# A two-layer hybrid decoder trunk on 8 cores: the first weight loads wait for input tiles, the operand sums stand in the order of use, and the planner's settings change

## The chip, the cores and the metric

The kernel runs on the 8 cores of one Trainium2 chip. A core has TensorE (PE, matrix products; PEld is its weight load), VectorE (DVE), ScalarE (ACT), GpSimd (POOL) and SyncE (SP), and 16 DMA engines that all queues of the core share. Each core computes 2 of the 16 sequences from start to end; nothing is exchanged between cores. The metric is the device time of the slowest core in microseconds (us); a lower number is better.

## The reference

```python
for l in range(DEPTH):                                   # DEPTH = 2
    x = x + 0.5 * swiglu(rms_norm(x, ffn1_norm[l]), ffn1_w1[l], ffn1_w3[l], ffn1_w2[l])
    x = x + token_mixing(rms_norm(x, mix_norm[l]), w_in[l], ...)
    x = x + 0.5 * swiglu(rms_norm(x, ffn2_norm[l]), ffn2_w1[l], ffn2_w3[l], ffn2_w2[l])

def rms_norm(x, g):
    return x * rsqrt(mean(x * x, axis=-1) + EPS) * g

def swiglu(h, w1, w3, w2):
    return (silu(h @ w1) * (h @ w3)) @ w2

def token_mixing(h, ...):
    u = h @ w_in
    # four groups of 256 columns: sparse attention (compressed, selected and
    # window branches), gated short convolution, window attention with sinks,
    # causal pooling; then a norm per group and
    return y @ w_out
```

The width is 1024, a sequence has 2048 tokens, the feed-forward width is 2816, x is float32.

## The kernel before

**Units.** The feed-forward work is cut into 16 units of 1024 tokens (sequence s, half u, layer l, which of the two feed-forwards fi). The list FL holds their order: units 0 to 3 are the four halves under the first feed-forward of layer 0. The mixer runs in 16 chunks of 512 tokens, woven into units 4 and later by the list MIX, and starts once units 0 and 1 have been recorded. A unit first normalises its two 512-token halves (`norm`: 8 input tiles of 128 features are loaded, squared on ACT at L630, summed on PE at L632 against ones, turned into a factor on ACT at L644 and L646, and scaled on DVE at L639).

**Products.** Every matrix product is made by a Strassen-like scheme of 7 products on quarters (`PROD`, L734) in the place of 8. Its operands are sums of quarters: `tops` (L713) makes t1 to t4 of the activations on DVE at L717, `wsum` (L677) makes the sums of the weights on DVE at L681. Product 1 and 2 need only activations of the first half; product 5 needs t1, which needs both halves. A `pair` (L738) takes two weight tiles (w1 and w3 of one q) and runs 14 products of 4 matmuls, 56 matmuls at L725; a unit has 11 pairs, then 4 `dcq` steps of 77 matmuls with three w2 tiles each, whose results POOL adds to yT in memory with an accumulating DMA (L824). So a unit is 11 x 56 + 4 x 77 = 924 matmuls at L725.

**Weights.** The weights lie in memory as float32. At its first use a tile is loaded by POOL's queue, which casts it to float16 (`prep`, L657 and L659), gets one DVE sum, and SP's queue stores it to a scratch tensor (L666); later units load it from there with SP (`wload`, L692). A tile is 128 x 2048 float16, 512 KB; pool "4" holds N4 of them at once. `PREP` = (a, b) says which share a/b of the tiles of a later feed-forward is prepared ahead, in the background of an earlier unit (`preps`, L1425); (0, 1) means none. Unit 0's w2 tiles are loaded, used and not stored; they are prepared again in unit 1.

**Start.** The first two norms load x by SP (L627, 256 KB each, 16 loads). `ycopy` (L1386) copies x to yT by SP, 512 KB each, 8 for a unit. Unit 0's first weight tile is asked for between its two norms; the next tiles as the pairs are recorded.

**What sets the order.** All operations are recorded by `op`, with their tiles, into a Graph. `schedule` then places them by a list planner: it takes the earliest-recorded ready operation of each engine, looks at most `ahead` operations past PE's front, hands out the slots of the pools, and holds a DMA back while more than `win` modelled bytes are under way (a wait for the landing of an earlier DMA is then built in). ACT stays with its current function table up to `hold` us. The result is one fixed, in-order list for each engine, with waits on semaphores between them. A waiting instruction stops everything behind it on its engine.

```python
                op("sp" if wide else "pool", lambda e, kc=kc: e.dma_start(out=xa(xf[kc]), in_=src[s, :, kc, c * 512:(c + 1) * 512]),
...
                        early["13", 0, 0] = mk("13", 0, 0)
```

## Time and profile before

| what | value |
|---|---|
| median of 3 runs | 4681.64 us (4676.58 to 4685.83) |
| the profiled execution, its time | 4662.98 us |
| its span, slowest of 8 cores (core 6) | 4661.9 us |
| spans of the 8 cores | 4636.2 to 4661.9 us |
| PE busy | 4518.3 us (97%) |
| DVE busy | 3088.4 us (66%) |
| ACT busy | 3050.7 us (65%) |
| PE idle in the first 40 us | 33.9 of 40 us |

A profile is one execution. Its time lies 18.7 us below the median of the three timed runs, so differences are worked out against the profile and then set against the median. In the rows below, "start us, us" are from the span's start; a bracket gives the engine's idle time before the instruction and what ended it; a window's row gives the busy time of each engine in that stretch, then the granted clock of PE as a share, the busy share of the 16 DMA engines and what they moved.

### The profile page before, as it was taken

What the parts mean: (1) busy time and instruction counts of PE and PEld (TensorE: products, weight loads), DVE (VectorE), ACT (ScalarE), POOL (GpSimd) and SP (SyncE); (2) the same over time, 40 slices, a digit from 0 to 9 for tenths busy, and PEclk for the clock granted to TensorE, in tenths of its full rate; (3) what the DMA queues carried; (4) which work ended last, traced back from release to release, by engine and by line L of the source; (5) the groups of instructions that cost most, each with busy time, mean ns of one, the idle gap of its engine ahead of it and who ended that gap; (6) DMA issues with size and microseconds to landing.
All of it is one profiled execution on the core that took longest, in us unless ns stands there. A gap on an engine that the chain in (4) does not pass through costs nothing.

```text
span 4661.9 us, 86720 instructions; the slowest of 8 cores (4636.2 to 4661.9 us)
## 1 busy us (share of the span) xinstructions
PE 4518.3 (97%) x25524; PEld 2101.8 (45%) x25524; DVE 3088.4 (66%) x7506; ACT 3050.7 (65%) x5742; POOL 874.4 (19%) x1282
## 2 busy tenths in 40 slices
PE   5899899999999999989999999999999999999999
PEld 2344444444444444444444444444444444444444
DVE  4656576667677667675757775766676767666663
ACT  3444577586877585867947666759585868585542
POOL 0011121111212112211122212111122221111101
PEclk9999999999999999999999999999999999999999
DMA  9998796767998759886588666664776898646554
GB/s 190 184 202 195 164 196 125 173 132 148 166 210 169 158 111 193 174 166 143 139 170 178 128 156 136 141 139 93 172 170 126 190 180 178 142 99 141 130 126 92
DMA packets 365404, 725.20 MB, mean 156 GB/s; under 512 B 37776, under 2 KB 145424, under 8 KB 364944
## 3 DMA queue, kind: packets, MB, share of 16 engines
q0 software_dynamic: 173904, 290.78, 44.3%
q1 hardware_dynamic: 191040, 428.87, 29.2%
q8 instruction: 218, 3.57, 0.3%
q14 instruction: 242, 1.98, 0.2%
HBM read 615.37 MB, written 256.43 MB: 187 GB/s over the span
## 4 chain that ended last, share of the span: by engine, by line
PE 85%; DMA 6%; DVE 4%; issue 3%; ACT 2%; POOL 0%; SPq 0%; DVEq 0%; ACTq 0%; POOLq 0%
PE ps L725 61%; PE ps L885 8%; PE ps L1167 4%; PE ps L1182 4%; PE ps L1195 2%; DMA yT<-M 2%; PE ps L632 1%; DMA M<-xT 1%; PE ps L1031 1%; DVE M L639 1%; DMA M<-s 1%; DMA M<-w2r 1%; DVE M L717 1%; PE ps L949 1%; PE ps L1276 1%
## 5 line engine op out<-in xcount | busy, mean ns | idle before, releaser
L725 PE MATMUL ps<-M 128*128 128x512 f16 x14784 | 3422.9, 380 | 54.5 <-DVE M L772 13.2
L725 PEld LDWEIGHTS ps<-M 128*128 128x128 f16 x14784 | 1409.0, 98 | 1730.8 <-issue 170.0
L681 DVE TENSOR_TENSOR M<-M 128x512 f16<-128x512 f16 (+1 forms) x1780 | 691.8, 412 | 130.7 <-DMA M<-s 53.8
L772 DVE TENSOR_TENSOR M<-M,ps 128x512 f16<-128x512 f32 x704 | 481.5, 685 | 435.6 <-PE ps L725 320.8
L824 POOL DMA_DIRECT2D yT<-M x464 | 400.3, 884 | 1697.2 <-ACT M L812 826.8
L776 ACT COPY M<-ps 128x512 f32<-128x512 f32 x704 | 410.1, 584 | 249.8 <-PE ps L725 241.7
L1185 ACT ACTIVATE M<-ps 128x512 bf16<-128x512 f32 x824 | 455.0, 603 | 51.0 <-PE ps L1182 47.1
L885 PE MATMUL ps<-M 128*128 128x512 f16 x1920 | 449.1, 380 | 8.9 <-DMA M<-hin 5.7
L732 ACT COPY ps<-ps 128x512 f32<-128x512 f32 x468 | 272.2, 582 | 213.1 <-PE ps L725 158.8
L717 DVE TENSOR_TENSOR M<-M 128x512 f16<-128x512 f16 x960 | 388.3, 424 | 34.3 <-DVE M L717 1.1
L764 DVE TENSOR_TENSOR M<-M,ps 128x512 f16<-128x512 f16 x352 | 240.9, 684 | 208.6 <-PE ps L725 206.5
L818 DVE SCALAR_TENSOR_TENSOR M<-ps,M 128x512 f32<-128x512 f32 x232 | 159.6, 689 | 279.2 <-PE ps L725 231.7
L812 ACT ACTIVATE M<-ps 128x512 f32<-128x512 f32 x232 | 138.7, 598 | 231.8 <-PE ps L725 225.5
L885 PEld LDWEIGHTS ps<-M 128*128 128x128 f16 x1920 | 184.7, 98 | 225.4 <-issue 13.8
L639 DVE SCALAR_TENSOR_TENSOR M<-M,GN 128x512 f16<-128x512 f16 (+1 forms) x384 | 265.2, 745 | 21.4 <-ACT M L646 21.2
L1182 PE MATMUL ps<-M 96*128 96x512 f16 x824 | 272.7, 380 | 2.0 <-DVE M L1215 0.9
L760 ACT ACTIVATE M<-M 128x512 f16<-128x512 f16 x352 | 219.1, 629 | 77.5 <-DVE M L772 76.0
L627 POOL DMA_DIRECT2D M<-yT x320 | 181.6, 608 | 458.5 <-PE ps L725 60.1
L756 ACT ACTIVATE M<-ps 128x512 f16<-128x512 f32 x352 | 209.5, 595 | 77.7 <-PE ps L725 74.2
L630 ACT ACTIVATE M<-M 128x512 bf16<-128x512 f16 (+1 forms) x384 | 228.1, 627 | 39.1 <-DMA M<-xT 34.8
L1195 PEld LDWEIGHTS ps<-M 128*128 128x128 bf16 x3296 | 173.8, 97 | 135.5 <-issue 26.4
L1167 PE MATMUL ps<-M 128*128 128x512 f16 x1024 | 233.7, 379 | 0.4 <-DVE M L1383 0.4
(152 smaller groups left out, 3903.2 us busy)
## 6 DMA issues: line engine op xcount, KB each, us to landing
M<-s SPq DMA_DIRECT2D x360, 512.0 KB, 5.8
yT<-M POOLq DMA_DIRECT2D x592, 256.0 KB, 9.3
s<-M SPq DMA_DIRECT2D x120, 512.0 KB, 7.8
M<-hin SPq DMA_DIRECT2D x210, 256.0 KB, 7.6
M<-w13r POOLq DMA_DIRECT2D x88, 512.0 KB, 11.9
M<-yT POOLq DMA_DIRECT2D x320, 128.0 KB, 7.0
M<-hout SPq DMA_DIRECT2D x112, 256.0 KB, 6.2
M<-w2r POOLq DMA_DIRECT2D x40, 512.0 KB, 8.3
```

Of the source, the lines that this page charges most:

```text
L639: op("dve", lambda e, d=dst[kc], gi=gi, x=xf[kc]: e.scalar_tensor_tensor(out=p1(d)[:, 0:512], in0=xa(x), scalar=GN[:, gi:gi + 1], in1=p2f( ...
L681: op("dve", lambda e, o_=o_, a_=a_, b_=b_, al=al: e.tensor_tensor(out=wap(W, o_, w), in0=wap(W, a_, w), in1=wap(W, b_, w), op=al), reads=[ ...
L717: op("dve", lambda e, o_=o_, x_=x_, y_=y_: e.tensor_tensor(out=p1(o_)[:, 0:512], in0=p1(x_)[:, 0:512], in1=p1(y_)[:, 0:512], op=ALU.subtract),
L725: r = e.matmul(ps(bk)[:], lhsT=wap(w, pos, 128, j * 128), rhs=p1(B[n, k0 + j])[:, 0:512], start=start and j == 0, stop=stop and j == nk - ...
L732: op("act", lambda e: e.copy(out=ps(dst)[:], in_=ps(src)[:]), reads=[src], writes=[dst], dur=0.57)
L772: op("dve", lambda e: e.tensor_tensor(out=p1(dst)[:, 0:512], in0=p2f(t), in1=ps(bk)[:], op=ALU.add), reads=[t, bk], writes=[dst], dur=t_dv ...
L776: op("act", lambda e: e.copy(out=p2f(t), in_=ps(bk)[:]), reads=[bk], writes=[t], dur=0.6)
L824: op("pool", lambda e: e.dma_start(out=yT[s, :, dc, t0:t0 + 512], in_=p2f(o), accum_op=ALU.add), reads=[o], writes=[kY[s][dc][2 * u + hf]] ...
L885: r = e.matmul(ps(bk)[:], lhsT=p2(t)[:, kc * 128:(kc + 1) * 128], rhs=p1(xn[kc])[:, 0:512], start=kc == 0, stop=kc == 7, skip_group_check= ...
L1167: r = e.matmul(ps(bk)[:], lhsT=p2(wo)[:, kc * 128:(kc + 1) * 128], rhs=yap(kc), start=n == 0, stop=n == 7, skip_group_check=True)
L1182: op("pe", lambda e: e.matmul(ps(sbk)[:], lhsT=kap(), rhs=p4(Q)[0:kk, b * 512:(b + 1) * 512], start=True, stop=True, skip_group_check=True ...
L1185: op("act", lambda e: e.activation(out=p1b(et)[:, 0:512], in_=ps(sbk)[:], func=AF.Exp, scale=0.125), reads=[sbk], writes=[et], dur=0.65, t ...
```

## The change

Four things. The first 16 weight loads get a `gate`, an extra dependency: the first waits for the landing of the sixth x load, the second for the twelfth, the others for the sixteenth. `tops` makes t3 and t1 of all four k first and then t2 and t4. PREP becomes (1, 3): every third tile of a later feed-forward is prepared one to four units ahead. And numbers of the planner change (pool sizes N1, N2, N4, look-ahead, window, hold, the modelled issue time of a weight load), so the whole order is made anew.

```diff
-        self.ahead = 400
+        self.ahead = 600
...
-        self.win = 5000000.0
+        self.win = 4000000.0
...
-        self.hold = 4.0
+        self.hold = 5.0
...
-    def op(self, eng, fn, reads=(), writes=(), dur=0.1, tbl=None, dma=0, after=(), prio=None, lat=0.0, look=None):
+    def op(self, eng, fn, reads=(), writes=(), dur=0.1, tbl=None, dma=0, after=(), prio=None, lat=0.0, look=None, gate=None):
...
+        if gate is not None:
+            deps.add(gate)
...
-N1, N2, N4, NS, NPF, NPX = 130, 20, 7, 24, 4, 4
-LOOKM, LOOKC = 250, 20
+N1, N2, N4, NS, NPF, NPX = 128, 19, 8, 24, 4, 4
+LOOKM, LOOKC = 250, 100
+XGATE = (5, 11, 15)
...
-MIX, PREP = ((2.0, 0.0), (5.0, 4.4), (14.4, 16.0)), (0, 1)
+MIX, PREP = ((2.0, 0.0), (5.0, 4.4), (14.4, 16.0)), (1, 3)
...
+                xloads.append(o)
...
-                op("pool", lambda e: e.dma_start(out=p4(t), in_=src), writes=[(t, (0, 1, 2, 3))], dur=0.8, dma=1048576)
+                op("pool", lambda e: e.dma_start(out=p4(t), in_=src), writes=[(t, (0, 1, 2, 3))], dur=0.6, dma=1048576, gate=gate)
...
-            for k in range(4):
-                tops(B, k)
+            tops(B, range(4))
             return B
 
-        def tops(B, k):
-            t3, t2, t4 = tile("1"), tile("1"), tile("1")
-            b11, b12, b21, b22 = (B[n, k] for n in ("11", "12", "21", "22"))
-            for o_, x_, y_ in ((t3, b22, b12), (b12, b12, b11), (t2, b22, b12), (t4, b21, t2)):
...
+        def tops(B, ks):
+            for k in ks:
+                B["t3", k], B["t2", k], B["t4", k] = tile("1"), tile("1"), tile("1")
+                B["t1", k] = B["12", k]
+            for names in (("t3", "t1"), ("t2", "t4")):
+                for k in ks:
+                    for o in names:
+                        x, y = dict(t3=("22", "12"), t1=("12", "11"), t2=("22", "t1"), t4=("21", "t2"))[o]
...
+                    gate = None
+                    if n == 0 and w == "13" and q < 8:
+                        gate = xloads[XGATE[min(2 * q + j, 2)]]
+                    return prep(l, fi, w, q, j, True, True, gate)
```

All other instructions keep their number: PE 25524, DVE 7506 and POOL 1282 in both kernels. SP issues 36 DMAs more, 24 loads of 512 KB and 12 of 384 KB from scratch (L692 before, L698 after): the tiles that PREP now prepares ahead.

POOL's queue at the start of the program, before. M4 is the pool of weight tiles, w13r the float32 weights; s1, s5, s8 and s10 are semaphores of landings, s31 the first of PE's.

```order
L599 MEMSET ZT 128x512 [waits barrier_Pool_Activation_PE_DVE_SP_gather]
L657 DMA M4<-w13r 128x2048 x3
L657 DMA M4<-w13r 128x2048 [waits s1]
L657 DMA M4<-w13r 128x2048 [waits s5]
L657 DMA M4<-w13r 128x2048 [waits s8]
L657 DMA M4<-w13r 128x2048 [waits s10]
L657 DMA M4<-w13r 128x2048 [waits s31,s34]
```

And after. s6 and s8 are the landings of the fourth and sixth x loads, s14 and s18 of the twelfth and sixteenth, s21 and s23 of the first and third copies of x to yT, s26 and s28 of the second and third weight loads, s30 of the first store of a weight tile.

```order
L602 MEMSET ZT 128x512 [waits barrier_Pool_Activation_PE_DVE_SP_gather]
L663 DMA M4<-w13r 128x2048 [waits s8,s6]
L663 DMA M4<-w13r 128x2048 [waits s18,s14]
L663 DMA M4<-w13r 128x2048 [waits s21]
L663 DMA M4<-w13r 128x2048 [waits s23]
L663 DMA M4<-w13r 128x2048 [waits s26]
L663 DMA M4<-w13r 128x2048 [waits s28]
L663 DMA M4<-w13r 128x2048 [waits s30]
```

Three weight loads went out at once before; now none goes out before six x loads have landed, and the second stands behind all sixteen.

SP's queue at the same place, before: M2<-xT are the x loads, s13<-M4 the stores of weight tiles, yT<-xT the copies.

```order
L593 DMA GN<-fnorm 128x48 [waits barrier_Pool_Activation_PE_DVE_SP_release]
L627 DMA M2<-xT 128x512 x5
L627 DMA M2<-xT 128x512 [waits s1]
L627 DMA M2<-xT 128x512
L627 DMA M2<-xT 128x512 [waits s5]
L627 DMA M2<-xT 128x512
L666 DMA s13<-M4 128x2048 [waits s2,s8]
L627 DMA M2<-xT 128x512 [waits s10]
L627 DMA M2<-xT 128x512 [waits s13]
L627 DMA M2<-xT 128x512 x5
```

And after:

```order
L596 DMA GN<-fnorm 128x48 [waits barrier_Pool_Activation_PE_DVE_SP_release]
L632 DMA M2<-xT 128x512 x15
L632 DMA M2<-xT 128x512 [waits s1]
L1396 DMA yT<-xT 128x1024 [waits s11,s8,s3]
L1396 DMA yT<-xT 128x1024 [waits s12,s10,s4]
L1396 DMA yT<-xT 128x1024 [waits s13,s5]
L1396 DMA yT<-xT 128x1024 [waits s16,s14,s6]
L1396 DMA yT<-xT 128x1024 [waits s18,s15,s7]
L672 DMA s13<-M4 128x2048 [waits s2,s25]
```

All sixteen x loads are now issued ahead of any store or copy; five copies follow them directly.

DVE from the program's start, before (L681 sums of weights, L639 scalings of the norm, L717 sums of activations):

```order
L592 MEMSET EPSB 128x1
L595 MEMSET ONES 128x128
L681 TENSOR_TENSOR M<-M 128x512 x20
L639 SCALAR_TENSOR_TENSOR M<-M,GN 128x512 x8
L681 TENSOR_TENSOR M<-M 128x512 x8
L764 TENSOR_TENSOR M<-M,ps 128x512
L639 SCALAR_TENSOR_TENSOR M<-M,GN 128x512 x8
L717 TENSOR_TENSOR M<-M 128x512 x16
```

And after (L687, L645 and L726 are the same three):

```order
L595 MEMSET EPSB 128x1
L598 MEMSET ONES 128x128
L645 SCALAR_TENSOR_TENSOR M<-M,GN 128x512 x10
L687 TENSOR_TENSOR M<-M 128x512
L645 SCALAR_TENSOR_TENSOR M<-M,GN 128x512
L687 TENSOR_TENSOR M<-M 128x512
L645 SCALAR_TENSOR_TENSOR M<-M,GN 128x512
L687 TENSOR_TENSOR M<-M 128x512 x2
L645 SCALAR_TENSOR_TENSOR M<-M,GN 128x512 x4
L726 TENSOR_TENSOR M<-M 128x512 x16
```

The sums of seven weight tiles stood around the two norms; now those of one tile stand among the scalings of the second half, and the sixteen sums of activations follow at once.

PE where the mixer's first chunk begins, before: L725 feed-forward products, L885 projections, L922 the bias of the compression, L949 the compression itself.

```order
L632 MATMUL ps<-M,ONES 128x512 x3
L725 MATMUL ps<-M 128x512 x31
L885 MATMUL ps<-M 128x512 x16
L989 MATMUL ps<-M,CB 128x512
L922 MATMUL ps<-PRB,M 128x1 x64
L949 MATMUL ps<-M 128x31 x64
L725 MATMUL ps<-M 128x512 x3
L969 MATMUL ps<-MS,PRB 128x32
```

And after (L733, L893, L930, L957 are those lines, L977 was L969):

```order
L638 MATMUL ps<-M,ONES 128x512
L733 MATMUL ps<-M 128x512 x27
L930 MATMUL ps<-PRB,M 128x1 x64
L893 MATMUL ps<-M 128x512 x8
L733 MATMUL ps<-M 128x512 x28
L957 MATMUL ps<-M 128x31 x64
L733 MATMUL ps<-M 128x512 x36
L977 MATMUL ps<-MS,PRB 128x32
```

Before, the steps of the chunk followed each other on PE with 3 feed-forward products among them; now 28 and 36 stand between.

## Rows read from the trace of the kernel before

**Rows 1.** The page: its first line, and the engines' busy time.

```profile
span 4661.9 us, 86720 instructions; the slowest of 8 cores (4636.2 to 4661.9 us)
...
PE 4518.3 (97%) x25524; PEld 2101.8 (45%) x25524; DVE 3088.4 (66%) x7506; ACT 3050.7 (65%) x5742; POOL 874.4 (19%) x1282
```

**Rows 2.** The chain that ended last, first 160 us: start, length, what.

```profile
11.25 27.73 DMA M<-xT
...
39.06 0.64 ACT M L630
...
44.93 5.12 PE ps L725 x12
...
68.75 9.48 PE ps L725 x32
```

**Rows 3.** The timelines of POOL, SP and ACT at the start, one after another.

```profile
1.63 2.39 POOL L657 DMA_DIRECT2D M<-w13r  x4
...
78.82 0.53 POOL L657 DMA_DIRECT2D M<-w13r  x1 [52.57 <-PE ps L725]
...
1.53 10.61 SPq L627 DMA_DIRECT2D M<-xT  x9
...
5.39 1.28 ACT L630 ACT_TABLE_LOAD   x1 [5.39 <-DMA M<-xT]
```

**Rows 4.** Windows of 4 us: PE busy, clock, DMA share, GB/s.

```profile
40.00:44.00 4.00, 1.00 (x2) 1.00 1.01 337
...
56.00:60.00 4.00, 1.36 (x5) 0.93 1.05 189
...
84.00:88.00 4.00, 4.00 (x20) 1.00 0.98 151
```

**Rows 5.** The timeline of DVE in the first 110 us.

```profile
29.44 1.82 DVE L681 TENSOR_TENSOR M<-M 128x512 f16<-128x512 f16 x4 [2.88 <-DMA M<-w13r]
...
59.19 5.39 DVE L639 SCALAR_TENSOR_TENSOR M<-M,GN 128x512 f16<-128x512 f32 x8 [3.37 <-ACT M L646]
64.50 5.45 DVE L717 TENSOR_TENSOR M<-M 128x512 f16<-128x512 f16 x16
```

**Rows 6.** The timeline of PE in the first 300 us.

```profile
134.78 67.50 PE L725 MATMUL ps<-M 128*128 128x512 f16 x312 [0.73 <-ACT ps L732]
211.12 5.28 PE L725 MATMUL ps<-M 128*128 128x512 f16 x12 [8.84 <-DVE M L772]
...
221.80 78.53 PE L725 MATMUL ps<-M 128*128 128x512 f16 x362
```

**Rows 7.** The chain that ended last, from 100 to 330 us.

```profile
185.64 23.36 DMA M<-w2r
```

**Rows 8.** DMA issues of the first 300 us: count, size, median us to landing.

```profile
yT<-xT SPq DMA_DIRECT2D x16, 512.0 KB, 19.2
...
M<-s SPq DMA_DIRECT2D x6, 512.0 KB, 8.6
```

**Rows 9.** Windows of 100 us: PE, PEld, DVE, ACT, POOL busy, clock, DMA share, GB/s.

```profile
0.00:100.00 100.00, 47.88 (x169) 17.86 (x170) 44.04 (x96) 32.83 (x52) 6.74 (x16) 0.91 0.91 186
100.00:200.00 100.00, 95.18 (x439) 42.27 (x438) 71.19 (x155) 52.30 (x94) 8.68 (x16) 1.00 0.94 203
200.00:300.00 100.00, 91.08 (x409) 40.28 (x408) 46.85 (x105) 27.04 (x44) 22.71 (x31) 0.95 0.96 155
300.00:400.00 100.00, 100.00 (x464) 45.17 (x463) 73.82 (x163) 57.28 (x101) 8.63 (x15) 1.00 0.85 222
400.00:500.00 100.00, 89.13 (x521) 41.49 (x519) 57.84 (x126) 29.87 (x52) 19.50 (x30) 0.95 0.97 207
...
600.00:700.00 100.00, 98.90 (x531) 45.36 (x530) 79.25 (x188) 68.49 (x142) 26.43 (x42) 1.00 1.01 210
```

**Rows 10.** The timeline of PE where the mixer begins.

```profile
491.52 1.69 PE L922 MATMUL ps<-PRB,M 64*128 64x1 f16 x61 [2.19 <-DMA M<-cw1r]
...
498.99 1.04 PE L949 MATMUL ps<-M 64*128 64x31 f16 x29 [4.68 <-issue]
```

More of the change, by code:

```diff
@@ L619, in build_program @@
         first = {}
+        xloads = []
         def norm(s, c, l, ni, dst, src):
@@ L626, in norm @@
             for kc in range(8):
-                op("sp" if wide else "pool", lambda e, kc=kc: e.dma_start(out=xa(xf[kc]), in_=src[s, :, kc, c * 512:(c + 1) * 512]),
+                o = op("sp" if wide else "pool", lambda e, kc=kc: e.dma_start(out=xa(xf[kc]), in_=src[s, :, kc, c * 512:(c + 1) * 512]),
                    reads=[kY[s][kc][c]], writes=[xf[kc]], dur=0.45 if wide else 0.6, dma=262144 if wide else XDMA, look=LOOKX)
+                xloads.append(o)
                 sq = tile("1")
@@ L647, in rstd, with prep @@
                reads=[rs], writes=[rs], dur=t_act(n), tbl="le")
-        def prep(l, fi, which, q, j, use, store=True):
+        def prep(l, fi, which, q, j, use, store=True, gate=None):
             t = tile("4", 4)
@@ L708, in ffn_operands @@
                 B["11", k], B["12", k], B["21", k], B["22", k] = xb[k][0], xb[k][1], xb[k + 4][0], xb[k + 4][1]
-            for k in range(4):
-                tops(B, k)
-            return B
-        def tops(B, k):
-            t3, t2, t4 = tile("1"), tile("1"), tile("1")
-            b11, b12, b21, b22 = (B[n, k] for n in ("11", "12", "21", "22"))
-            for o_, x_, y_ in ((t3, b22, b12), (b12, b12, b11), (t2, b22, b12), (t4, b21, t2)):
-                op("dve", lambda e, o_=o_, x_=x_, y_=y_: e.tensor_tensor(out=p1(o_)[:, 0:512], in0=p1(x_)[:, 0:512],
-                                                                         in1=p1(y_)[:, 0:512], op=ALU.subtract),
-                   reads=[x_, y_], writes=[o_], dur=t_dve(512, True))
-            B["t1", k], B["t2", k], B["t3", k], B["t4", k] = b12, t2, t3, t4
+            tops(B, range(4))
+            return B
+        def tops(B, ks):
[6 more added lines that the diff above has]
+                        x, y = dict(t3=("22", "12"), t1=("12", "11"), t2=("22", "t1"), t4=("21", "t2"))[o]
+                        op("dve", lambda e, o_=B[o, k], x_=B[x, k], y_=B[y, k]: e.tensor_tensor(
+                            out=p1(o_)[:, 0:512], in0=p1(x_)[:, 0:512], in1=p1(y_)[:, 0:512], op=ALU.subtract),
+                           reads=[B[x, k], B[y, k]], writes=[B[o, k]], dur=t_dve(512, True))
         def prod(bk, w, pos, B, n, k0, nk, start, stop):
@@ L799, in pair @@
                 H["11", i], H["12", i], H["21", i], H["22", i] = h[0], h[1], h[2], h[3]
-                tops(H, i)
+                tops(H, (i,))
             def dcq(i, G):
@@ L1469, in mk @@
                     inscr.add((l, fi, w, q, j))
-                    return prep(l, fi, w, q, j, True)
+                    gate = None
+                    if n == 0 and w == "13" and q < 8:
+                        gate = xloads[XGATE[min(2 * q + j, 2)]]
+                    return prep(l, fi, w, q, j, True, True, gate)
                 if B is None:
```

## The prediction

> **What bounds the kernel now.** I read the page first: PE is busy 4518.3 of 4661.9 us, so all idle time of PE together is 143.6 us, and nothing that leaves PE's work alone can bring more than that and a little clock [rows 1]. Then the windows of 100 us: 52.1 us of the idle time lie in the first 100 us alone, another 13.7 in the next 200, 10.9 between 400 and 500 [rows 9]. So the reader is to look at the start, and for what ends its waits. The chain of waits says it: one x load takes 27.73 us from its issue to its landing; the first products start at 44.93, and the run of products without a long gap at 68.75 [rows 2]. The timelines say why: POOL sends four weight loads at 1.63 us, in the same microseconds in which SP sends the x loads, and both share the 16 DMA engines [rows 3]. PE has the weights long before it has the operands: the next weight load goes out only at 78.82, 52.57 us after the one before, when PE has at last used up a tile [rows 3]. A second thing to see is that the DMA engines are nearly full for 500 us: busy shares 0.91, 0.94, 0.96, 0.85 and 0.97 [rows 9].
>
> **The x loads first.** While x loads make up nearly all traffic, the engines move 337 GB/s [rows 4]; a load of 262,144 bytes is then 0.78 us. The first lands at 5.39 us in any case (ACT's first instruction waits for it) [rows 3]. The other fifteen then land by 5.4 + 15 x 0.78 = 17.1 us if nothing shares the engines. The gate lets one weight load in among them (the second waits for the sixteenth x load as well); a weight tile of 524,288 bytes by itself moves at 151 GB/s [rows 4], 3.5 us. So the last x lands between 17.1 and 20.6; I take 19, since the weight load needs some microseconds before its data move and some x loads are through by then. The far bound is a load like the 27.73 us one [rows 2], issued at 11: 39 us.
>
> From there to the dense products: from the last square of the first half (39.06) to the first product is 5.87 us [rows 2], in which sum, factor and four scalings lie; four more scalings at 5.39/8 = 0.67 are 2.7 us; the four sums of the first weight tile, now among them on DVE, 1.82; and eight of the sixteen sums of activations, 5.45/2 = 2.73 [rows 5]. Together 13.1 us, so 32.1 in the place of 68.75: **36.6 us earlier**. The new order of `tops` is in it: t1 of all four k is ready after 8 instructions, where it took 14; 6 x 0.34 = 2.0 us, and only here, because later units make these sums under the products of the unit before. The weights' own side holds: the first tile goes out at some 9 us, the second at 19, the third and fourth behind the first and third copy of x, at 189 GB/s [rows 4] 2.8 us each alone and about double beside a weight load, so at some 23 and 33 us. Tiles three and four are wanted at 32 + 12 = 44 us, a pair being 56 matmuls at 78.53/362 = 0.217 us [rows 6]. The wait that replaces the old one is POOL's: behind the gated load stand only other weight loads, and they are late by design.
>
> **What the DMA engines take back.** The gain moves PE forward, not the bytes. Unit 0 ended at 288.6 us: 616 of its 924 products stand before the run at 221.80, 308 x 0.217 = 66.8 after [rows 6]. From 68.75 that is 219.9 us; with the start at 32.1 and the same 219.9 it would end at 252. The engines were busy 0.91 + 0.94 + 0.96 of the first 300 us, 281 us [rows 9]; of that, work for unit 1 were 8 copies and 6 loads from scratch [rows 8], at most 14 x 2.8 = 39 us. So unit 0 needs at least 242 us of a full DMA, and at the 0.94 of before 258: 6 us given back. Up to 500 us the sum is 463 us of DMA work [rows 9]; the fullest window of the five ran at 0.97, and by that rate the same work takes 477. So of 36.6 us only **22.7** are left by then; at 0.99 it would be 32, at the mean of before, 0.926, nothing. I take 0.97, because an engine list that asks earlier keeps the queues fuller, and PE no longer leaves them idle for want of free tiles. After 500 us I see no second giving back: what is early stays early.
>
> The Trainium skill (DMA: Bandwidth & Descriptors, Specifications) gives a core about 358 GB/s of memory traffic. By that figure, an estimate from it: unit 0 reads and writes some 73 MB (16 + 16 x loads, weights as float32, stores, copies counted twice, accumulations counted twice), 203 us, the DMA engines would never bind, all 36.6 us would stay and the sum below would be 45 us. The trace speaks against it: in the window from 56 us the engines were busy at 1.05 while 189 GB/s moved [rows 4], and full engines, not memory's limit, are what the next transfer waits for.
>
> **The mixer's start.** PE idles 10.9 us between 400 and 500 and runs at a mean clock of 0.95 there [rows 9]; 2.19 of it waits for a compression weight, 4.68 is an issue gap between the small matmuls [rows 10]. The new order puts 28 and 36 feed-forward products between the steps of that chain, so waits for data there are covered; the issue gap need not go. Bounds: nothing, and 10.9 + 5 us of clock. I take **8**.
>
> **The rest.** Background tiles: 36 more loads from scratch, 16.5 MB more on 725; their float32 loads and stores are moved, not added, away from the units that use the tiles first. An eighth slot in the pool of weight tiles, one slot less in another, longer holding of a table: they re-deal the small gaps of the remaining 4,150 us. The nearest rows for the gaps are single waits of 1 to 9 us, as the 8.84 before 211.12 [rows 6], and I have no reason for a sign: 0, between -8 and +8 us.
>
> **The sum.** 22.7 + 8 = 30.7 us. The profiled execution took 4662.98; less 30.7 it is 4632.3. The median of the runs is 18.7 above the profiled one; I leave that distance: 4681.6 - 30.7 = **4651 us**. About 0.2%, 9.4 us, is what a measurement of this kernel can tell from no change.
>
> **The rivals.** *The DMA engines take back all of it.* If they can't be fuller over 500 us than 0.926, x lands early, the weights of the first pairs land late, and PE waits among the pairs for what it no longer waits for before them. For it: five windows in a row at 0.85 to 0.97 [rows 9]; against it: they idled for want of free tiles, as POOL's 52.57 us wait shows [rows 3]. Only the mixer's 8 us are left: 4674, a chance of 0.17.
>
> *Nothing is taken back.* Stores and copies that are deferred go into slack behind 500 us, the 36.6 us stay, and the mixer's start gives the full 15.9: 52.5 us, 4629. For it: stores need not land for PE to go on as long as slots are free, and there are eight; against it the same windows. 0.15.
>
> *Slower: the background tiles stop DVE.* Each tile prepared ahead puts a sum on DVE's in-order list that waits for a float32 load; behind it stand the additions that free PE's banks. Before, one late w2 tile (23.36 us from issue to landing) cost PE 8.84 us [rows 6, 7]. There are 36 such tiles now in stretches that had none, and one of these, 600 to 700 us, has a DMA share of 1.01 already [rows 9]. At 8.84 us each, four late ones cancel the gain, and five make it 44 - 31 = 13 us slower: 4695. It decides from one late tile in seven on. Against it: a planner with 600 operations of look-ahead asks for these tiles long before the sum. 0.08.
>
> **How the numbers follow.** Forecast 0.60, all taken back 0.17, nothing taken back 0.15, slower 0.08. The likeliest is 4651. The range 4622 to 4676 takes in 4629 less 7 us for the re-dealt gaps and nearly all of the rival at 4674; outside are the slower case and the tails, some 0.19. Faster by over 0.2% (under 4672): forecast, nothing taken back, and 0.07 of the first rival, 0.82. Within: 0.10. Slower: 0.08.
>
> **What would show it.** Right: x loads of under 3 us each in their landing distance, the dense products from 30 to 36 us, POOL's first weight load near 9 us, unit 0's 924th product between 252 and 265, DMA shares near 0.97 up to 500, and a PE idle time in the first 500 us of some 45 us in the place of 77. Wrong: PE waiting for DVE's weight sums (L687) behind loads of w13r between 60 and 200 us says that the DMA engines bind more than I took; a sum of PE's idle time after 600 us that differs by more than 10 us from before says that the rest of the order, which I put at nothing, decides.

## The result and the profile after

The changed kernel takes 4613.4 us (median; 4610.61 to 4616.2) against 4681.3 (4676.58 to 4685.83): a ratio of 0.9855, interval 0.9836 to 0.9874. (One more run of it was disturbed; with that one the median reads 4614.79.) The direction was forecast, the size was not: some 68 us, where 30.7 stood in the prediction, and 4613 lies below its range. The profiled execution of after took 4616.2 us, 46.8 less than that of before.

The page of after: its first line, the engines' busy time, and the costliest group (busy, mean ns, idle before). They answer to [rows 1].

```profile
span 4614.9 us, 86879 instructions; the slowest of 8 cores (4598.9 to 4614.9 us)
...
PE 4533.8 (98%) x25524; PEld 2106.5 (46%) x25524; DVE 3089.6 (67%) x7506; ACT 3027.1 (66%) x5722; POOL 874.0 (19%) x1282
...
L733 PE MATMUL ps<-M 128*128 128x512 f16 x14784 | 3445.1, 382 | 35.7 <-ACT ps L740 8.5
```

PE's idle time fell from 143.6 to 81.1 us. At the same time its busy time rose by 15.5 us for the same 25524 instructions, so a part of the idle time came back as a lower clock. ACT has 20 instructions fewer (5722 against 5742), all of them loads of a function table, so the sentence of the change that all others keep their number holds for PE, DVE and POOL. (Lines of after stand a few higher: L733 is L725 of before, L687 was L681, L726 was L717, L645 was L639, L893 was L885.)

The start. The chain that ended last of after, first 100 us (answers to [rows 2]):

```profile
13.41 18.85 DMA M<-xT
...
32.35 0.64 ACT M L636
...
44.88 55.29 PE ps L733 x210
```

POOL's timeline of after (answers to [rows 3]), and behind it PE's:

```profile
13.78 0.70 POOL L663 DMA_DIRECT2D M<-w13r  x1 [12.19 <-DMA M<-xT]
32.89 0.55 POOL L663 DMA_DIRECT2D M<-w13r  x1 [18.42 <-DMA M<-xT]
```

```profile
33.50 1.91 PE L733 MATMUL ps<-M 128*128 128x512 f16 x4
36.32 1.87 PE L733 MATMUL ps<-M 128*128 128x512 f16 x4 [0.91 <-ACT ps L740]
44.88 15.38 PE L733 MATMUL ps<-M 128*128 128x512 f16 x58 [6.69 <-DVE M L726]
```

The gate does what it says: POOL's first load waits for x, and the products run from 44.88 instead of 68.75. But the last x load, issued at 13.41, takes 18.85 us. The landings, read off the trace: the first x tile at 5.57 us, the sixth at 13.07, the twelfth at 17.88, and the last four at 20.43, 25.68, 29.53 and 32.27.

Windows of 4 us of after (PE, PEld, DVE, ACT, POOL busy; clock, DMA share, GB/s) say where the last four go; they answer to [rows 4]:

```profile
8.00:12.00 4.00, 2.08 (x5) 0.41 (x4) 0.00 (x0) 1.97 (x4) 0.00 (x0) 1.00 1.01 240
...
24.00:28.00 4.00, 0.59 (x1) 0.10 (x1) 0.13 (x1) 0.63 (x1) 0.00 (x0) 1.00 0.85 169
```

With x loads alone, full engines move 240 GB/s over these 4 us. Once the first weight load (issued 13.78, landed 26.39) and the copies to yT (SP issues three behind the last x load, landed by 36.61) share the engines, it is 169, at a busy share of 0.85.

Windows of 100 us of after, which answer to [rows 9]:

```profile
0.00:100.00 100.00, 69.71 (x239) 25.94 (x240) 52.53 (x114) 37.66 (x62) 7.78 (x18) 0.91 0.94 194
100.00:200.00 100.00, 100.00 (x382) 41.43 (x381) 66.15 (x144) 41.12 (x72) 8.37 (x15) 0.81 0.90 188
200.00:300.00 100.00, 97.88 (x432) 42.85 (x431) 53.23 (x117) 33.40 (x58) 22.57 (x31) 0.96 1.01 178
300.00:400.00 100.00, 97.67 (x452) 43.76 (x451) 70.26 (x156) 54.56 (x98) 6.55 (x13) 1.00 0.81 220
400.00:500.00 100.00, 96.24 (x493) 43.35 (x491) 54.02 (x116) 31.59 (x53) 22.59 (x32) 0.98 0.95 184
```

The second row is what nobody would look for. PE is busy for all 100 us and yet issues 382 instructions, where before it issued 439 in 95 us [rows 9]. The granted clock is 0.81, which is neither of TensorE's two levels (0.5 is 1.2 GHz, 1.0 is 2.4 GHz). In this execution all eight cores have it, for 158.6 to 160.9 us from 54 to 56 us on. So the engine does not wait for data there; it runs more slowly.

The rest of the program, in four long windows, first of before, then of after:

```profile
500.00:2000.00 1500.00, 1472.69 (x8638) 689.90 (x8638) 1025.17 (x2576) 1085.00 (x2064) 314.10 (x469) 0.99 0.79 162
2000.00:2100.00 100.00, 88.29 (x460) 39.87 (x459) 72.36 (x159) 55.54 (x106) 19.15 (x26) 0.91 0.77 161
2100.00:4600.00 2500.00, 2479.07 (x14182) 1160.37 (x14181) 1685.61 (x4103) 1701.34 (x3216) 462.11 (x664) 1.00 0.67 145
```

```profile
500.00:2000.00 1500.00, 1481.74 (x8778) 696.85 (x8775) 1048.23 (x2631) 1097.22 (x2112) 315.87 (x473) 1.00 0.82 175
2000.00:2100.00 100.00, 98.97 (x530) 46.98 (x528) 67.31 (x153) 47.39 (x90) 21.76 (x28) 1.00 0.80 175
2100.00:4600.00 2500.00, 2483.71 (x14198) 1162.07 (x14197) 1676.50 (x4078) 1682.96 (x3178) 465.57 (x669) 1.00 0.68 146
```

Behind 500 us PE idled 27.3 + 11.7 + 20.9 = 59.9 us before, and 18.3 + 1.0 + 16.3 = 35.6 after. That is 24 us less in a part for which the prediction had put nothing, and 10.7 of it in one window of 100 us, where the clock rose from 0.91 to 1.00 besides.

Setting both traces side by side by the amount of PE work done (counted in the us that the products would take at full clock; mean of the eight cores), after is ahead of before by 21.8 us at the very start, 9.3 around 160 us, 4 to 5 from 330 to 480, 15 once the mixer has begun, 20 to 22 from 900 to 1950, 36.4 behind the unit boundary at 2040 and 37 to 42 from 2550 to the end. So of 42 us, about 5 come from the start, 10 from the mixer's start and 27 from the rest. A second profile of the kernel before (e1 below) is 9 us faster than the first; against it the same split is 1, 8 and 24.

### The profile page after: what moved, and what is told of

Read it like the earlier page. It is cut to its first block, busy times and chain, and to the rows that moved or that the text cites. A ratio compares the mean times of both kernels' runs of the same rounds, so it can differ in the third digit from the quotient of the medians.

```text
span 4614.9 us, 86879 instructions; the slowest of 8 cores (4598.9 to 4614.9 us)
## 1 busy us (share of the span) xinstructions
PE 4533.8 (98%) x25524; PEld 2106.5 (46%) x25524; DVE 3089.6 (67%) x7506; ACT 3027.1 (66%) x5722; POOL 874.0 (19%) x1282
## 4 chain that ended last, share of the span: by engine, by line
PE 86%; DMA 5%; DVE 3%; issue 2%; ACT 2%; SPq 0%; POOL 0%; DVEq 0%; ACTq 0%; POOLq 0%
PE ps L733 61%; PE ps L893 8%; PE ps L1175 5%; PE ps L1190 4%; PE ps L1203 2%; PE ps L638 1%; DMA M<-s 1%; PE ps L1039 1%; DMA M<-xT 1%; DMA yT<-M 1%; DMA yT<-xT 1%; PE ps L1284 1%; PE ps L957 1%; DVE M L645 1%; DMA hcw<-M 1%
## 5 line engine op out<-in xcount | busy, mean ns | idle before, releaser
L733 PE MATMUL ps<-M 128*128 128x512 f16 x14784 | 3445.1, 382 | 35.7 <-ACT ps L740 8.5
L733 PEld LDWEIGHTS ps<-M 128*128 128x128 f16 x14784 | 1414.7, 98 | 1728.3 <-issue 235.7
L687 DVE TENSOR_TENSOR M<-M 128x512 f16<-128x512 f16 (+1 forms) x1780 | 692.3, 413 | 107.8 <-DMA M<-s 39.3
L1193 ACT ACTIVATE M<-ps 128x512 bf16<-128x512 f32 x824 | 456.9, 602 | 57.3 <-PE ps L1190 48.1
L893 PE MATMUL ps<-M 128*128 128x512 f16 x1920 | 447.2, 379 | 1.7 <-ACT PBIAS L934 0.9
L726 DVE TENSOR_TENSOR M<-M 128x512 f16<-128x512 f16 x960 | 387.9, 424 | 33.4 <-DVE M L726 0.3
L645 DVE SCALAR_TENSOR_TENSOR M<-M,GN 128x512 f16<-128x512 f16 (+1 forms) x384 | 264.7, 746 | 40.2 <-ACT M L652 40.2
L893 PEld LDWEIGHTS ps<-M 128*128 128x128 f16 x1920 | 184.6, 98 | 219.0 <-issue 6.3
```

The lines of the kernel that those rows point to most:

```text
L645: op("dve", lambda e, d=dst[kc], gi=gi, x=xf[kc]: e.scalar_tensor_tensor(out=p1(d)[:, 0:512], in0=xa(x), scalar=GN[:, gi:gi + 1], in1=p2f( ...
L687: op("dve", lambda e, o_=o_, a_=a_, b_=b_, al=al: e.tensor_tensor(out=wap(W, o_, w), in0=wap(W, a_, w), in1=wap(W, b_, w), op=al), reads=[ ...
L726: op("dve", lambda e, o_=B[o, k], x_=B[x, k], y_=B[y, k]: e.tensor_tensor(out=p1(o_)[:, 0:512], in0=p1(x_)[:, 0:512], in1=p1(y_)[:, 0:512] ...
L733: r = e.matmul(ps(bk)[:], lhsT=wap(w, pos, 128, j * 128), rhs=p1(B[n, k0 + j])[:, 0:512], start=start and j == 0, stop=stop and j == nk - ...
L893: r = e.matmul(ps(bk)[:], lhsT=p2(t)[:, kc * 128:(kc + 1) * 128], rhs=p1(xn[kc])[:, 0:512], start=kc == 0, stop=kc == 7, skip_group_check= ...
L1193: op("act", lambda e: e.activation(out=p1b(et)[:, 0:512], in_=ps(sbk)[:], func=AF.Exp, scale=0.125), reads=[sbk], writes=[et], dur=0.65, t ...
```

## The experiments

The theory to test was formed from these traces: the start gives some 24 us that a lower clock takes back, and most of the lasting gain is the remade order of the instructions, with the background tiles the chief suspect. Its rival is that the gates do nearly everything, now or by shifting what follows. In the expectations below, "work 20" is 20 us of PE work as counted above, and an order that is "dealt anew" is the same work that an edit made the planner place in another order.

Since the 0.81 stretch comes and goes, times alone compare badly. Two readings are steadier. One is the *full-speed time*: each core's span times its mean granted clock, averaged over the cores (the table has the median of the runs behind the ratio). The medians of repeats of one kernel agree within some 3 us, its single executions within 7 to 9; the first profiled execution of before, 4615, lies above all later ones (4604 to 4612), so the effects below are taken against e1. It undervalues a removed wait around which the clock had fallen. The other is PE's idle time, summed from the trace up to the last product, mean of eight cores; two profiles of before differ by 3 to 4 us in it. A 0.81 stretch lowers it before 500 us, since a slower PE waits less for data.

| kernel | ratio to before (interval) | PE idle before 500 us | PE idle after 600 us | cores with a 0.81 stretch of some 160 us | full-speed time |
|---|---|---|---|---|---|
| before | 1 | 75.2 | 53.4 | 0 | 4615 (one execution) |
| e1 before again | 1.000 (0.9976-1.0024) | 71.2 | 50.6 | 0 | 4609 |
| e2 gates alone | 0.9965 (0.9948-0.9982) | 60.4 | 51.0 | 0 | 4601 |
| e3 numbers alone | 0.9991 (0.9962-1.002) | 56.4 | 56.4 | 2 | 4607 |
| e7 background alone | none | 62.8 | 46.5 | 6 | 4599 |
| e14 sums alone | 0.9995 (0.9957-1.0033) | 69.5 | 52.0 | 2 | 4608 |
| e13 before, hold 5 | 1.0011 (0.9981-1.0041) | 68.2 | 58.7 | 4 | 4618 |
| after | 0.9855 (0.9836-0.9874) | 35.2 | 34.0 | 8 | 4571 |
| e5 after again | 0.981 (0.9769-0.9852) | 36.2 | 32.6 | 8 | 4570 |
| e9 after, third | 0.9843 (0.9795-0.9892) | 38.1 | 33.1 | 4 | 4572 |
| e4 after, no gates | 0.9899 (0.9859-0.994) | 57.3 | 32.9 | 0 | 4590 |
| e10 the same again | 0.9896 (0.9854-0.9939) | 56.5 | 32.7 | 2 | 4588 |
| e6 after, no background | 0.9937 (0.9888-0.9986) | 35.8 | 56.3 | 8 | 4589 |
| e8 after, old sums | 0.9874 (0.9825-0.9924) | 37.5 | 42.4 | 6 | 4580 |
| e15 after, N1 127 | 0.9887 (0.9823-0.995) | 45.7 | 36.2 | 2 | 4575 |
| e11 after, copies wait | 0.9835 (0.9793-0.9878) | 38.5 | 31.7 | 4 | 4573 |
| e16 the same again | 0.9851 (0.9797-0.9905) | 41.1 | 32.5 | 2 | 4573 |

**Both kernels again.** No edit.

> The kernel before, unchanged, with a profile of its own in the same session as the next three. Theory S (the gain of the change is the start: x lands first, dense products 24 us earlier): nothing to tell here, ratio 1.000 within 0.002. Theory O (most of the gain is the order of the rest, remade): the same. What it settles is the distance of 18.7 us between the first profile (4663) and the timed runs (4677 to 4686): if the difference lies between sessions, this profile's execution lies with its own timed runs, and its cores show at which place of the program the extra time stands (a granted clock under 1 over a long stretch after the start would be one cause).

> The changed kernel, unchanged, in the same session as the next three, to be set beside the one without gates (ratio 0.9899 there). Theory C (the gates bring 20 us at the start, and a stretch of some 160 us with a granted clock of 0.81 right after it takes them back): the 0.81 stretch shows again on most cores, the ratio is 0.983 to 0.989, and the profile with gates ends within 10 us of the one without. Theory S (the gates are worth 20 us at the end too): no such stretch on most cores, ratio 0.980 to 0.985.

> The changed kernel once more, in one session with the next three, as their measure. Span times granted clock, the core's time in full-speed terms, was 4566 to 4570 us in the session before (the kernel before: 4605 to 4612 in both sessions). Theories C and S: the same again within 4 us, with a stretch of 160 us at a granted clock of 0.81 from about 54 us on most cores.

Before repeats; after repeats in time, full-speed time and idle time. The third one is the most telling run of the study, because four of its cores have the 0.81 stretch and four have not, in one execution of one program. Windows of 50 us, core 0 and then core 3:

```profile
150.00:200.00 50.00, 50.00 (x192) 20.77 (x191) 32.88 (x74) 21.34 (x38) 4.14 (x7) 0.81 0.88 195
200.00:250.00 50.00, 49.19 (x217) 21.53 (x215) 31.63 (x69) 16.71 (x30) 10.43 (x14) 0.94 1.02 169
```

```profile
150.00:200.00 50.00, 50.00 (x233) 22.57 (x232) 37.83 (x83) 26.65 (x47) 5.03 (x8) 1.00 1.00 211
200.00:250.00 50.00, 43.24 (x190) 18.48 (x188) 21.92 (x50) 7.80 (x14) 12.42 (x18) 0.93 0.99 164
```

From 150 to 200 the fast core does 233 matmuls against 192. Then it meets the DMA engines at 0.99 and idles 6.8 us. Of the gap between the two kinds of cores 14.2 us are left at the work that takes 233 us on the fast ones, and 12 at the end. Other executions of e9 put it higher: 19 us between cores with mean clocks of 0.992 to 0.993 and of 0.998 to 0.999 in one of them, and 21 between an execution with 0.991 to 0.992 on all cores and one with 0.996 to 0.998 on all (that one took 4592.4 us). So a stretch that takes 0.19 x 160 = 30 us of clock costs 12 to 21 us of time at this place, because the rest would have been waits.

**The gates alone, and after without them.** In before, the gates are put in; in after, they are taken out.

```diff
...
+                    if n == 0 and w == "13" and q < 8:
+                        gate = xloads[XGATE[min(2 * q + j, 2)]]
...
```

> The kernel before with the gates on the first sixteen weight loads alone; sums, background tiles and planner numbers as before. Theory S: dense products start at 45 to 48 us in the place of 69, the first 500 us end 15 to 24 us earlier, the time falls by 20 to 35 us (ratio 0.992 to 0.996). Theory O: the early start is given back by 500 us and the later places (2040 us, 2390 us) look like the kernel before, so the time falls by at most 8 us (ratio 0.998 to 1.000).

> The changed kernel without the gates, all else as in it. Theory S: dense products start near 65 us again and the time rises from 4615 by 20 to 35 us (ratio to before 0.990 to 0.993). Theory O: it rises by at most 10 us (ratio 0.985 to 0.988).

> The changed kernel without the gates, beside the one with them on the same chip. Theory C: full-speed time 20 us more than with gates (4586 to 4592), but without the 0.81 stretch on most cores, so that the time itself is within 10 us of the changed kernel. Theory S: the time is 15 to 25 us longer than with gates, too.

Alone the gates bring 0.35% (0.18 to 0.52) and 8 us of full-speed time, between what the two theories gave them; in after they are worth 16 to 19. Of the times themselves, e4's profile (no core with the stretch) took 4609.6, less than the 4616.2 of after, and e10's (two cores with it) 4632.5 against 4611.7 of e9, so times alone do not settle it. The idle times say where they work: before 500 us they take 11 us from before and 19 from after (13 by the four cores of e9 without the low clock, 43.6 against 57). After 600 us they change nothing: 51.0 against 50.6, 33 against 33. Where the gain of the gates alone goes, PE's timeline of e2 shows:

```profile
204.74 1.86 PE L731 MATMUL ps<-M 128*128 128x512 f16 x4 [5.53 <-DMA M<-w2r]
214.38 45.87 PE L731 MATMUL ps<-M 128*128 128x512 f16 x205 [7.78 <-DMA M<-w2r]
```

The gates put it 22 us ahead of e1 at the work that e1 reaches at 164 us, and 9 ahead at 252: the w2 tiles of unit 0 land late, and the early PE waits for them. This is the prediction's giving back, seen clean, at full clock.

**The copies wait too.** The first unit's copies of x get the gate of the last x load.

```diff
-               writes=[kY[s][i][2 * u], kY[s][i][2 * u + 1]], dur=0.45, dma=524288)
+               writes=[kY[s][i][2 * u], kY[s][i][2 * u + 1]], dur=0.45, dma=524288, gate=xloads[15] if (s, u) == (0, 0) else None)
```

> The changed kernel with the first unit's copies of x to yT held until the sixteenth x load has landed as well. Theory X (the dense products start at 45 and not at 32 because copies and a weight load share the engines with the last four x loads): the last x lands at 20 to 23 us in the place of 32, dense products from 34 to 37 us; by work 100 some 8 us ahead of the changed kernel in full-speed terms. Theory D (the DMA engines give none of that away, total bytes bind): back to within 3 us of the changed kernel by work 260.

> The changed kernel with the copies held back, once more. Full-speed time was 4569 to 4577 and the time 4596 to 4617, against 4564 to 4573 and 4592 to 4618 for the changed kernel beside it. Theory D (the DMA engines bind until 260 us, so an earlier start is given back): full-speed time within 5 us of the changed kernel again. Theory X (a better kernel): 4565 or less.

On core 3 of e16 the last x load lands at 28.0, not 32.3 and not the 20 to 23 that were expected, and a second weight load now runs beside it (issued at 18.29). At the first 20 us of work it is 4 us ahead of after; at the work that after reaches at 457 us it is 2.5 behind (cores without the low clock), and the full-speed time is the same, 4573 against 4572. The runs lie at 4596 to 4617; nothing here shows a better kernel. What the start gains beyond after is taken back by waits: on the four cores of e16 with complete records and without the low clock PE waits 6 to 9 us between 60 and 180 us, nearly all for DVE's and ACT's work on its results, and 5 to 12 for w2 tiles behind that; on three such cores of e9 it is 0 to 4 and 6 to 10.

**The numbers, hold alone, and a mere new deal.** In before all the planner's new numbers; then of these only hold; in after one slot less in pool 1.

```diff
-        self.ahead = 400
+        self.ahead = 600
...
-        self.win = 5000000.0
+        self.win = 4000000.0
...
-        self.hold = 4.0
+        self.hold = 5.0
...
-N1, N2, N4, NS, NPF, NPX = 130, 20, 7, 24, 4, 4
-LOOKM, LOOKC = 250, 20
+N1, N2, N4, NS, NPF, NPX = 128, 19, 8, 24, 4, 4
+LOOKM, LOOKC = 250, 100
...
```

```diff
-N1, N2, N4, NS, NPF, NPX = 128, 19, 8, 24, 4, 4
+N1, N2, N4, NS, NPF, NPX = 127, 19, 8, 24, 4, 4
```

> The kernel before with the planner's numbers of the changed kernel alone (look-ahead, window, hold, pool sizes, modelled issue time); no gates, old order of the sums, no background tiles. Theory S: no gain beyond the re-dealt gaps, ratio 0.998 to 1.002. Theory O: the gaps at the mixer's start, at 830 us and at 2040 us go, 25 to 45 us less (ratio 0.990 to 0.995), with dense products still starting at 69 us.

> The kernel before with the planner's hold at 5 in the place of 4 alone: the order is dealt anew, nothing else changes. Theory R (re-dealing by itself moves the time as much as the edits seemed to): full-speed time more than 10 us off the 4605 to 4612 of before, either way. Theory E (the edits did it): within 6 us.

> The changed kernel with one slot less in the pool of small tiles (127 for 128): all edits stay, the order is dealt anew. Theory R: full-speed time more than 10 us off the 4566 to 4573 of the changed kernel. Theory E: within 6 us, the time within 12 of the changed kernel's 4610.

The numbers alone change no time, but they do not do nothing: 15 us less idle before 500, 3 to 6 more after 600. Where the mixer begins they bring what after has there: by work e3's lead over e1 goes from 5 to 16 us, while it does not rise in e2, e7 and e14. Behind 1000 us it is lost again (the small table below). Hold alone costs 9 us of full-speed time, between the two theories; one slot costs 4, within theory E. So a new deal of the same work moves the kernel by 4 to 9 us for no reason that was looked for, and a part whose effect is no larger cannot be told from it.

**The background tiles.** Taken out of after; put into before.

```diff
-MIX, PREP = ((2.0, 0.0), (5.0, 4.4), (14.4, 16.0)), (1, 3)
+MIX, PREP = ((2.0, 0.0), (5.0, 4.4), (14.4, 16.0)), (0, 1)
```

> The changed kernel with no background tiles (PREP back to (0, 1)), all else as in it. Theory P (preparing every third tile ahead takes DMA work off the units that use them first, and that is most of the gain after 500 us): the time rises by 20 to 35 us from the changed kernel, and PE waits return near 2040 us; ratio to before 0.992 to 0.997. Theory N (it is the planner's numbers and the chance order): within 10 us of the changed kernel, ratio 0.984 to 0.988.

> The kernel before with PREP (1, 3) alone: every third tile of a later feed-forward prepared ahead, all else as before. Theory P: 20 to 35 us less than before (ratio 0.9925 to 0.9955), the gain between 700 and 2500 us of the span. Theory N: within 8 us (0.998 to 1.002). Theory of the slower case of the prediction (sums of late tiles stop DVE): slower, ratio over 1.002, with DVE waits on loads of w13r and w2r growing.

Without them after loses the whole late gain, nearly what theory P said: 56.3 us idle after 600, more than before had, and 18 us of full-speed time. Alone, in before, they bring less than P said, 4 to 7 us of idle time there and 9 to 10 of full-speed time (its six runs took 4661 to 5430 us and gave no ratio; the fastest two took 4661.2 and 4666.7).

PE's idle time by stretch of the span, summed from the traces (us, mean of the six cores whose records are complete), says where:

| stretch | e1 before | e3 numbers alone | e7 background alone | e6 after, no background | e9 after |
|---|---|---|---|---|---|
| 600 to 1000 | 6.6 | 2.1 | 7.6 | 1.7 | 2.4 |
| 1000 to 1900 | 12.4 | 20.0 | 12.6 | 20.8 | 11.4 |
| 1900 to 2100 | 12.2 | 10.7 | 6.9 | 11.0 | 1.6 |
| 2100 to the last product | 17.2 | 21.9 | 17.1 | 20.8 | 15.8 |

The new numbers win 4 to 5 us before 1000, with the tiles or without. Without the tiles they then lose 8 us up to 1900 and 4 to 5 behind 2100. The tiles take both losses away, and at the unit boundary near 2040 they win 9 us beside the new numbers, 5 beside the old ones. So neither part brings the late gain alone.

At the unit boundary one sees how. Before, DVE's timeline and then PE's:

```profile
2042.19 10.69 DVE L639 SCALAR_TENSOR_TENSOR M<-M,GN 128x512 f16<-128x512 f16 x16
2052.79 5.45 DVE L717 TENSOR_TENSOR M<-M 128x512 f16<-128x512 f16 x16
```

```profile
2044.93 0.38 PE L1378 MATMUL ps<-M,ONES 128*128 128x512 bf16 x1 [1.59 <-ACT M L1377]
2050.99 3.57 PE L885 MATMUL ps<-M 128*128 128x512 f16 x8 [5.68 <-DMA M<-hin]
2056.23 2.09 PE L949 MATMUL ps<-M 64*128 64x32 f16 x64 [1.67 <-ACT M L932]
```

e6, without the tiles, DVE and PE of core 4:

```profile
2027.03 5.39 DVE L645 SCALAR_TENSOR_TENSOR M<-M,GN 128x512 f16<-128x512 f16 x8
2032.33 5.45 DVE L726 TENSOR_TENSOR M<-M 128x512 f16<-128x512 f16 x16
2037.69 0.62 DVE L687 TENSOR_TENSOR M<-M 128x384 f16<-128x384 f16 x2
```

```profile
2038.47 1.44 PE L733 MATMUL ps<-M 128*128 128x512 f16 x3 [8.55 <-DVE M L687]
```

e3, with the new numbers and no tiles, PE of core 4, has the same wait (L681 is L687 there):

```profile
2027.44 1.44 PE L725 MATMUL ps<-M 128*128 128x512 f16 x3 [8.54 <-DVE M L681]
```

And after, DVE and PE:

```profile
2011.11 1.56 DVE L687 TENSOR_TENSOR M<-M 128x512 f16<-128x512 f16 x5
2012.58 6.05 DVE L645 SCALAR_TENSOR_TENSOR M<-M,GN 128x512 f16<-128x512 f16 x9
...
2024.38 5.46 DVE L726 TENSOR_TENSOR M<-M 128x512 f16<-128x512 f16 x16
```

```profile
2020.37 4.70 PE L733 MATMUL ps<-M 128*128 128x512 f16 x21
2024.90 1.89 PE L893 MATMUL ps<-M 128*128 128x512 f16 x8
```

At a boundary DVE has 11 to 16 us of scalings and sums for the next unit. If the weight sums of the current one stand behind them in its list, PE stops: 8.55 us in e6. Where tiles were prepared long ago there are products left to run, and PE has no bracket of more than 0.23 us through the same work in after (2000 to 2030). Before has another wait there. In the 150 us from 1950 it loads 11 tiles as float32 (three of w13, eight of w2) and 3 from scratch and stores 13, its loads of hin take 9.0 us in the median, and PE waits 5.68 us for one; after loads 4 as float32 and 15 from scratch and stores 4, and hin takes 4.4. The bytes moved are the same, 24.8 and 24.7 MB. In e6 (core 5), with hin at 5.9, PE does not wait for it. That the tiles are needed is shown. That they do it by these two ways, DVE's list and fewer float32 loads and stores, is read from the traces and was not tested apart.

**The order of the operand sums.** The old order of `tops` in after; the new one in before.

```diff
-            for names in (("t3", "t1"), ("t2", "t4")):
-                for k in ks:
...
+            for k in ks:
+                for o in ("t3", "t1", "t2", "t4"):
...
```

> The changed kernel with the sums of the activations in the old order (all four of one k, then the next k). Priced at 2 us at the start, nothing elsewhere: theories S and C both 2 us slower than the changed kernel at work 20 of the start, and at the end within 8 us of it, since the order is dealt anew. If the new order matters at each of the units whose operands are made without cover, it is 10 to 20 us slower.

> The kernel before with the sums of the activations in the order of use alone; the order of everything else stays but for some fifty rows. Priced at 2 us at the start: dense products 2 us earlier, full-speed time 0 to 3 us less. If the 10 us by which the changed kernel lost with the old sums belong to the sums: 8 to 12 us less, at the units whose operands are made without cover (69 us and 2040 us of the span).

Alone it brings 1 us, at the start (80.0 against 80.8 at the first 20 us of work), half of what was priced. In after the old order costs 9, and behind 600 us all its added idle time lies between 1000 and 1900, 21.7 us against 11.4 in e9. The longest wait there, 4.64 us on core 7 before the products at 1682, is once more for a weight sum that stands behind sums of activations on DVE. Whether the order of the sums put it there or the new deal did, which moves as much, is not settled here.

**A busy PE from the first norm on.** 128 products of zeros, unused, between the squares of the first two norms, to see whether a PE that is already busy is spared the low clock.

```diff
+                if wide and (s, c) == (0, 0) or wide and (s, c) == (0, 1):
+                    wb = bank()
+                    for _ in range(8):
+                        op("pe", lambda e, wb=wb: e.matmul(ps(wb)[:], lhsT=ZT[:, 0:128], rhs=ZT[:], start=True, stop=True, skip_group_check=True),
+                           reads=[sq, kZT], writes=[wb], dur=0.22)
```

> The changed kernel with eight matmuls on zeros behind each of the sixteen squares of the first two norms, so that PE works at some 40 to 60% from 6 us to 33 us; their results are not used. Theory W (the 0.81 stretch follows a jump from an idle PE to a dense one): it goes, or is gone before 100 us, on most cores, and the time falls by 15 to 25 us. Theory L (it follows the dense run itself): 160 us at 0.81 from about 50 us as before, time within 8 us of the changed kernel.

Inconclusive. Cores 0 and 1 ran at 0.81 from 13 and 11 us on, cores 2 and 3 from 65, cores 4 to 7 not at all before 500 us; the order was dealt anew besides, with 101 us of idle time after 600. Its seven runs took 4747 to 5457 us and gave no ratio.

## Why the prediction was wrong, point by point

**The bound and the place.** Right: the start is bound by x and then by the DMA engines, and the gain there is of the forecast's order.

**The x loads first: 36.6 us earlier. Mis-sized.** The last x load was to land at 17.1 to 20.6, and landed at 32.3. Two numbers failed. SP's issues were counted as free; but nine of them took 10.61 us before [rows 3], and in after the sixteenth went out only at 13.41, where by 0.78 us each eleven loads should have landed. And the rate of 337 GB/s came from one window of 4 us [rows 4]; in after full engines move 240 to 283 up to 16 us, and 169, at a share of 0.85, once the weight load and the copies, which were left out at this place, share them. The far bound of 39 us was the useful one. The rest of the step held: from the last x to the dense products 13.1 us were worked out, and 12.6 passed. POOL's first load went at 13.8, not 9. The start came 24 us earlier.

**What the DMA engines take back: 22.7 left. Right where the clock is full, wrong in most runs.** On the four cores of e9 without the low clock unit 0 ends at 257.6 to 267.5, mean 263.0 (forecast 252 to 265; before 283.9 and 280.4 in two profiles), PE idles 43.6 us before 500 (forecast some 45), core 3 has DMA shares of 0.94 to 1.02 in four of the five windows, and 16 to 21 us of the start are left at the work that takes 457 us. The forecast's mechanism there, PE early and waiting for w2 tiles, is what e2 shows. With the low clock unit 0 ends at 274 to 283, and of the start some 5 us are left against the first profile of before, 1 against e1. That cause stood nowhere in the prediction. The ceiling of memory did not set the time alone. The Trainium skill (DMA: Bandwidth & Descriptors, Specifications) has some 358 GB/s for a core, by which, as an estimate, unit 0 would have taken 203 us. Core 3 took 263, with its engines at 1.01 and 1.00 from 100 to 300 us. But the prediction read too much into the 189 GB/s of [rows 4]: the profile counts the bytes that a transfer writes (a weight tile counts 512 KB, half of its float32 source), and the window held stores and copies within memory, so memory saw between 189 and 378. By the sizes and landings of core 3, with copies, accumulations and casting loads counted at what they read and write, memory saw some 320 GB/s from 100 to 200 us, an estimate, where the windows show 221. Whether a packet of a full engine waits for the engine or for memory no run here tells.

**The mixer's start: 8 us. Right:** 9 to 12 by work, whichever profiles are paired. e3 shows that the new numbers bring it, and in its order, too, feed-forward products stand between the steps of the chain; there an issue gap of 2.05 us was left of the 4.68 [rows 10].

**The rest: nothing, within 8 us. The step that failed:** it was 24 to 27 us. I took the small gaps behind 600 us for a sum of accidents, and looked at single waits rather than where they stood. What stood there instead were three effects that the runs tell apart: the numbers win 4 to 5 us of idle time before 1000, the tiles win 9 at the boundary near 2040 beside the new numbers, and they keep those numbers from losing 12 elsewhere (e3, e6, e7). (The 36 loads added 17.3 MB, 742.5 against 725.2 on the pages, not 16.5.) The prediction's own windows of 100 us end at 700. One more row at 2000 shows PE idle 11.7 us at a clock of 0.91, at a unit boundary, and a third of the later tiles was to be taken out of just such places. The sign that the prediction named for this failure, idle time after 600 us that differs by more than 10 us, came true: 53.4 against 34.0. Clock comes on top: behind gaps of some microseconds stand stretches at half clock (0.5, the 1.2 GHz level). Over the whole span they cost 33 to 35 us of clock in before and 5 to 9 in the three profiles of after; behind 600 us it is 13 to 15 and 3 to 4.

**The distance of 18.7 us between profile and runs, kept: wrong.** In the later runs beside the experiments before took 4648 to 4660 us in runs with all cores at a mean clock of 0.991 or more, and 4668 to 4714 in those with a pair of neighbouring cores at 0.979 to 0.989: about what one or two 0.81 stretches make. The profile of before was of the first kind; that its timed runs were of the second is likely from their times, not shown. After's profile had the stretch itself and is the slowest of its three runs. Like with like: 4592 against 4648 to 4660 without any stretch, 4607 to 4618 against 4668 to 4714 with. So of the 68 us between the medians the profiles hold 47; the other 21 are before's 18 and the 3 us by which the profile of after lies above its median.

**The rivals.** *All taken back, 4674*: false in the time, though with the low clock 1 to 5 us of the start's 24 were all that was left. *Nothing taken back, 4629*: the time is nearer, but by luck, since 3 to 8 us of the start were taken back at full clock and 19 or more at the low one, and the time came from the rest. *Slower, background tiles stop DVE*: refuted, and the other way round, since e6 lost 18 us without them. I had costed the sums that are added early and not those that vanish late.

**What stays open.** By full-speed time the four parts alone bring 8 + 2 + 10 + 1 = 21 us, and together 38. Gates and background tiles are each worth 16 to 19 within after. Tiles and numbers need each other, as the small table shows; which of the numbers it is, the eighth slot or the longer look-ahead, was not tried, and 4 to 9 us of any such figure may be the deal.

## What to carry to other kernels

Go through the whole span in windows before a term is set to nothing, and look at the unit boundaries for a full engine whose list holds two units' work. When several settings change at once, compare them stretch by stretch: the numbers alone look neutral, and are a gain and a loss. Work that is prepared ahead is to be costed where it vanishes as well as where it appears. Before a load's landing is forecast, count the issues ahead of it on its queue and everything else that is released in the same microseconds.

## What was not expected of the hardware

A granted clock of 0.81 for 158 to 166 us, with PE all but full, on pairs of neighbouring cores (0 and 1, 2 and 3, and so on), which begins for both of a pair within a few tenths of a microsecond to two. The two profiles of before have none, but variants of it do (e3, e7, e13, e14), and not only at the start: windows of e13, core 5:

```profile
2360.00:2380.00 20.00, 17.77 (x197) 10.59 (x195) 4.89 (x14) 5.07 (x16) 4.86 (x6) 0.83 1.03 215
...
2400.00:2500.00 100.00, 99.46 (x475) 41.76 (x474) 64.15 (x188) 73.58 (x125) 17.37 (x26) 0.81 0.49 103
```

There it runs from 2380.4, 4 us behind a stretch at half clock; in e10 from 109.1, 9 us behind one; in after from 54.0, 9 us behind the first dense products. In these three it follows PE's return from a wait. It can last longer: on cores 0 to 3 of e12 the same level held for up to 1415 us. What sets it off, and why one pair has it and the next has not, no run here tells.
